# Finishing and storing each projection tile behind its own norms in a two-layer hybrid decoder step

## The reference, cut to what matters

```python
def project(xn, pos, p):
    z = xn @ p['w_in']                       # 1088 x 1024 by 1024 x 2448
    qa, ka, va, fa, glu_in, qc, kvc, gc, ud, vd = jnp.split(z, SPLIT_IDX, axis=-1)
    qa = rmsnorm(qa, p['fox_qn_g']);  ka = rmsnorm(ka, p['fox_kn_g'])
    logf = jax.nn.log_sigmoid(fa + p['fox_bf'])
    glu = ga * jax.nn.sigmoid(gb)
    qc = rope(rmsnorm(qc, p['nsa_qn_g']), pos)
    keys = rope(rmsnorm(kvc[:, :, 0::2], p['nsa_kn_g']), pos)
    gc = jax.nn.sigmoid(gc)
...
o_a = fox_prompt(qa, ka, va, logf)           # attention with a running sum of logf
o_b = conformer_conv(glu, ...)               # 31 taps along the rows, channel by channel
o_c = nsa_prompt(qc, gc, kvc, p)             # compressed, selected and window attention
o_d = gmlp_gate(ud, vd, p)                   # u * (lower triangle of ws @ layernorm(v) + bs)
y = merge_and_ffn(x, (o_a, o_b, o_c, o_d), p)
```

## Time and profile before

| | us |
|---|---|
| median of 3 runs | 4176.93 (4174.57 to 4179.18) |
| the profiled execution | 4181.78 |
| its span in the trace | 4179.9 |
| PE busy in the span | 3425.3 (82%) |
| DVE busy | 1442.6 (35%) |
| ACT busy | 977.6 (23%) |
| mean granted clock of PE | 0.911 |

### The profile page before, as it was taken

The page is one execution under the profiler, slowest core; times in us unless marked ns, Lnnn a source line. Parts: engine busy times, 40 slices in busy tenths (PEclk is TensorE's granted clock), DMA queues, the critical chain, the costliest instruction groups (busy, mean ns, idle before and its releaser), DMA issues.

```text
span 4179.9 us, 56173 instructions
## 1 busy us (share of the span) xinstructions
PE 3425.3 (82%) x22454; PEld 1933.6 (46%) x22454; DVE 1442.6 (35%) x2646; ACT 977.6 (23%) x1745; POOL 165.7 (4%) x136
## 2 busy tenths in 40 slices
PE   6987848888357999999988885688882779999998
PEld 3444436566223444444444443466661334444444
DVE  2555433333442321232127454333344333212311
ACT  2111114444222320121011111244442122102301
POOL 0111110000000000000001111000000000000000
PEclk8998869999778999999999897799996889999999
DMA  6322162332210121111072223433303111201211
GB/s 209 90 69 87 46 174 79 112 127 75 89 42 25 45 65 30 37 54 50 20 203 63 75 72 92 118 127 112 125 23 102 33 32 49 61 20 50 60 50 43
DMA packets 407740, 317.19 MB, mean 76 GB/s; under 512 B 158493, under 2 KB 389562, under 8 KB 400186
## 3 DMA queue, kind: packets, MB, share of 16 engines
q1 hardware_dynamic: 400490, 213.65, 18.5%
q0 software_dynamic: 7072, 101.19, 6.9%
HBM read 272.27 MB, written 51.84 MB: 78 GB/s over the span
## 4 chain that ended last, share of the span: by engine, by line
PE 65%; SPq 8%; DVE 8%; issue 7%; ACT 5%; DMA 5%; POOL 1%; POOLq 0%; DVEq 0%; ACTq 0%
PE PS L887 39%; PE PS L977 5%; PE PS L1240 4%; PE PS L1221 4%; PE PS L905 3%; PE PS L1122 2%; PE PS L879 2%; DMA out_fox_logf_p<-arena 2%; POOL arena L2360 1%; SPq L710 1%; PE PS L967 1%; PE PS L1163 1%; PE PS L1254 1%; ACT arena L1424 1%; SPq L705 1%
## 5 line engine op out<-in xcount | busy, mean ns | idle before, releaser
L887 PE MATMUL PS<-arena 128*128 128x512 bf16 (+1 forms) x10368 | 1634.7, 319 | 74.9 <-DVE arena L1698 40.0
L887 PEld LDWEIGHTS PS<-arena 128*128 128x128 bf16 x10368 | 789.5, 98 | 919.5 <-issue 93.3
L977 PE MATMUL PS<-arena 128*128 128x512 f32 (+3 forms) x1152 | 482.1, 574 | 0.9 <-ACT arena L1399 0.9
L1375 ACT ACTIVATE arena<-arena 128x1024 bf16<-128x1024 f32 (+1 forms) x112 | 145.5, 1301 | 1268.7 <-PE PS L887 1155.5
L2268 DVE TENSOR_TENSOR arena<-PS,arena 128x1088 f32 (+1 forms) x48 | 62.1, 1293 | 778.2 <-PE PS L887 778.2
L977 PEld LDWEIGHTS PS<-arena 128*128 128x128 f32 (+1 forms) x1152 | 208.8, 185 | 239.0 <-issue 204.5
L1969 DVE TENSOR_REDUCE arena<-PS 128x1 f32<-128x1024 f32 (+5 forms) x192 | 138.8, 724 | 379.4 <-PE PS L1224 379.3
L1221 PE MATMUL PS<-arena 128*128 128x512 f32 (+3 forms) x576 | 231.5, 509 | 5.7 <-ACT arena L1489 4.4
L2301 DVE SCALAR_TENSOR_TENSOR arena<-PS,arena 128x1088 f32<-128x1088 f32 x64 | 82.7, 1293 | 388.6 <-PE PS L887 388.6
L1240 PE MATMUL PS<-arena 128*128 128x64 f32 x1632 | 216.5, 279 | 0.0
L1240 PEld LDWEIGHTS PS<-arena 128*128 128x128 f32 x1632 | 204.1, 197 | 8.3 <-issue 5.0
(11 more groups left out here) (311 smaller groups left out, 2784.8 us busy)
## 6 DMA issues: line engine op xcount, KB each, us to landing
arena<-in_w_ff SPq DMA_DIRECT2D x64, 512.0 KB, 4.1
arena<-in_w_ff SPq DMA_DIRECT2D x32, 1024.0 KB, 5.6
arena<-in_cache_nsa_kv SPq DMA_DIRECT2D x256, 64.0 KB
x_s<-arena SPq DMA_DIRECT2D x2, 4352.0 KB, 18.1
arena<-x_s SPq DMA_DIRECT2D x2, 4352.0 KB, 13.3
arena<-in_w_in SPq DMA_DIRECT2D x4, 2048.0 KB, 11.6
arena<-in_w_out SPq DMA_DIRECT2D x16, 512.0 KB, 4.2
arena<-o_s SPq DMA_DIRECT2D x48, 128.0 KB, 2.4
```

Source lines behind the costliest of these rows:

```text
L887: last = mm(PS[:, 1536 * k + a:1536 * k + a + wd], ww[:, c, :], xx[:, c, a:a + wd], start=c == 0 and n == 0, stop=c == blocks - 1 and n == 2)
L977: last = mm(PS[0:r, c * 512:c * 512 + b - a], XNT[:, j, t * P:t * P + r], Wt[:, j, a:b], start=j == 0, stop=j == KD - 1)
L1375: run(WH[k][:, 0:blocks, :], WF[k][:, 0:blocks, :], ACT.Copy).then_inc(S["w_hi"], 1)
```

## The change

Six edits, as the diff shows them:

1. DVE's step for tile t becomes `norm_rows(t)`, `finish(t)`. PE's `small(t - 1)` moves from the end of its step t to the middle, between the product and the transposes of that step's two pieces, and ACT's `compressed_in(t - 1)` and some wait counts follow it.
2. SP stores tile t in step t. The store of `y_s` is put ahead of tile 7's stores.
3. ACT's waits for the stores and for `fin` move from the head of the tile to the instruction ahead of which they stand now.
4. Two of a tile's three taps go between the row sums and the wait for the fourth chunk in `norm_rows`, the third goes into `rstd`, where DVE waits for POOL.
5. The four loads of keys and values become one load of `KV4` with runs of 1 KB, and the gate load goes behind head 0's loads. Transposes, `KTS` and the value products read and write that layout.
6. `fox_in(0)` moves ahead of the barrier, behind waits for `y_out` and for the last piece product.

```diff
@@ layout
-        KK = lo.take(QT * 2 * HD, t=QT, g=2, d=HD)
-        VV = lo.take(QT * 2 * HD, t=QT, g=2, d=HD)
-        KTS = [x.rearrange("p t g d -> p (t g d)") for x in (KK[:, 0:QT // 2], KK[:, QT // 2:QT])]
+        KV4 = lo.take(QT * 4 * HD, t=QT, g=4, d=HD)
+        KTS = [KV4[:, 4 * n:4 * n + 4, 0:3:2, :] for n in range(2)]
@@ SP
                 def store_step(t, k, m):
-                    if not (isinstance(t, int) and t == 0):
-                        store_tile(t - 1, 1 - k)
+                    if t == QT - 1:
+                        sp.wait_ge(S["conv_done"], CW)
+                        sp.dma_start(y_s, Yc.rearrange("p c n -> p (c n)")).then_inc(S["y_out"], 16)
+                    store_tile(t, k)
 
                 each_tile(store_step)
-                sp.wait_ge(S["conv_done"], CW)
-                sp.dma_start(y_s, Yc.rearrange("p c n -> p (c n)")).then_inc(S["y_out"], 16)
-                store_tile(8, 0)
...
-                for dst, first in ((KK, 2), (VV, 3)):
-                    for g in range(2):
-                        sp.dma_start(dst[:, :, g, :], kvc_s[0:SEQ, first + 2 * g, :].rearrange("(t p) d -> p t d", p=P)).then_inc(S["kv4_in"], 16)
+                sp.dma_start(KV4.rearrange("p t g d -> p t (g d)"),
+                             kvc_s[0:SEQ, 2:6, :].rearrange("(t p) g d -> p t (g d)", p=P)).then_inc(S["kv4_in"], 16)
+                head_in(0)
                 sp.dma_start(GH, g_s[0:SEQ].rearrange("(t p) c -> p t c", p=P)).then_inc(S["gate_in"], 16)
-                head_in(0)
@@ PE
                     if t < QT:
-                        pe.wait_ge(S["raw_ev"], 2 * (2 * t + 4) if t < QT - 1 else 2 * PIECES + 1)
+                        pe.wait_ge(S["raw_ev"], 2 * (2 * t + 3) if t < QT - 1 else 2 * PIECES + 1)
...
-                    if p >= 4:
-                        pe.wait_ge(S["cp_ev"], p // 2 - 1)
+                    if p >= 3:
+                        pe.wait_ge(S["cp_ev"], (p - 1) // 2)
...
                         elif t < QT and c == 2:
                             piece_mm(2 * t)
+                            if t:
+                                small(t - 1, 1 - k)
                             piece_T(2 * t + 1)
+                        elif t == QT and c == 2:
+                            small(t - 1, 1 - k)
...
-                    if t:
-                        small(t - 1, 1 - k)
@@ ACT
-                    if t >= 2:
-                        act.wait_ge(S[f"st{k}"], 176 * m)
-                        act.wait_ge(S["fin"], t - 1)
...
                     out(0, SQ[0:r, 0:512], 0, 512, ACT.Square)
+                    if t >= 2:
+                        act.wait_ge(S[f"st{k}"], 176 * m)
                     out(1, VB[k][0:r, :], 0, 260)
...
                     out(2, SQ[0:r, 764:1152], 0, 388, ACT.Square)
+                    if t:
+                        compressed_in(t - 1)
                     if t < QT:
                         piece_out(2 * t + 1)
+                    if t >= 2:
+                        act.wait_ge(S["fin"], t - 1)
                     out(3, UV[k][0:r, :], 0, 512)
...
-                    if t:
-                        compressed_in(t - 1)
@@ DVE
-            def rstd(out, sums, count, which, n):
+            def rstd(out, sums, count, which, n, meanwhile=None):
                 V.tensor_scalar(out, sums, 1.0 / count, EPS, ALU.mult, ALU.add).then_inc(S[f"{which}_mean"], 1)
+                if meanwhile:
+                    meanwhile()
                 dve.wait_ge(S[f"{which}_rstd"], n)
...
                     V.reduce_sum(SS18[0:r, 0:18], SQ[0:r, :].rearrange("p (g d) -> p g d", d=HD), AX)
+                    taps = list(range(FIRST_TAPS + t * TAPS, min(CW, FIRST_TAPS + (t + 1) * TAPS)))
+                    for j in taps[:-1]:
+                        conv(j)
...
-                    rstd(SS18[0:r, :], SS18[0:r, :], HD, "row", t + 1)
+                    rstd(SS18[0:r, :], SS18[0:r, :], HD, "row", t + 1, lambda: [conv(j) for j in taps[-1:]])
...
                     norm_rows(t, k, m)
-                    if t:
-                        finish(t - 1, 1 - k)
-                    for j in range(FIRST_TAPS + t * TAPS, min(CW, FIRST_TAPS + (t + 1) * TAPS)):
-                        conv(j)
+                    finish(t, k)
@@ POOL
                 G.tensor_scalar(piece_rows, piece_rows, POOL * PIECES, None, ALU.add)
+                pool.wait_ge(S["y_out"], 16)
+                pool.wait_ge(S["kvc_mm"], PIECES + 1)
+                fox_in(0)
                 everyone()
...
-                fox_in(0)
                 pool.wait_ge(S["suf_out"], 16 * NB)
```

More of the change, by code:

```diff
@@ L1028, in extra @@
                     if what == "kv":
-                        transposes(key, KK[:, :, key[1] // 2, :], HD, key[1] % 2)
+                        transposes(key, KV4[:, :, key[1] // 2 * 2, :], HD, key[1] % 2)
                     elif what == "q":
@@ L1138, in request @@
                             for c in range(4):
-                                last = mm(out[32 * c:32 * (c + 1), 0:P], QNALL[:, b, :], KTS[s % 2][:, c * P:(c + 1) * P],
+                                last = mm(out[32 * c:32 * (c + 1), 0:P], QNALL[:, b, :], KTS[s % 2][:, c],
                                           start=True, stop=True)
@@ L1189, in merged @@
                     last.then_inc(S["pt_T"], 1)
-                pe.wait_ge(S["kv4_in"], 64)
+                pe.wait_ge(S["kv4_in"], 16)
                 for n in range(4):
@@ L1238, in values @@
                     for n, j in enumerate(js):
-                        v = {"fox": VF[h % 2][:, j, :], "sel": VV[:, j, 0, :], "win": VV[:, j, 1, :]}[kind]
+                        v = {"fox": VF[h % 2][:, j, :], "sel": KV4[:, j, 1, :], "win": KV4[:, j, 3, :]}[kind]
                         last = mm(PS[:, at:at + HD], PTR[u % 2][:, n * P:(n + 1) * P], v,
@@ L1496, in request_out @@
                         n = key[2]
+                        src = group_bank(key)
                         dst = KTF[n // 2 % 2][:, n % 2, :] if n < 8 else KTS[n % 2]
-                        run(dst, group_bank(key), ACT.Copy).then_inc(S["pt_evA"], 1)
+                        if n >= 8:
+                            src = src.rearrange("p (t g d) -> p t g d", t=4, g=2)
+                        run(dst, src, ACT.Copy).then_inc(S["pt_evA"], 1)
                     elif key[2] < 2:
@@ L1887, in _ @@
                 each_tile(z_step)
-                finish(8, 0)
                 dve.wait_ge(S["kvc_mm"], PIECES + 1)
@@ L2158, in _ @@
                 V.memset(MX, -3e38)
-                dve.wait_ge(S["gate_in"], 16)
                 for key in GROUPS[:10]:
@@ L2166, in _ @@
                     h, v = u // UH_, u % UH_
-                    if v == 0:
+                    if v == 4:
+                        dve.wait_ge(S["gate_in"], 16)
                         V.tensor_copy(GU[h % 2][:, :, 1:3], GH[:, :, 3 * h + 1:3 * h + 3]).then_inc(S["dve_done"], 1)
@@ L2386, in _, with fox_in @@
                 G.tensor_scalar(piece_rows, piece_rows, POOL * PIECES, None, ALU.add)
+                def fox_in(b):
+                    G.indirect_dma_start(KVP[b % 2].rearrange("p r n -> p (r n)"), None,
+                                         A["cache_fox_kv"].rearrange("l n (q r) c h d -> (l n q) (r c h d)", r=NPG),
+                                         bass.IndirectOffsetOnAxis(block_rows[:, b:b + 1], 0)).then_inc(fox_in_sem[b % 2], 16)
+                pool.wait_ge(S["y_out"], 16)
+                pool.wait_ge(S["kvc_mm"], PIECES + 1)
+                fox_in(0)
                 everyone()
@@ L2400, in _ @@
                 pool.wait_ge(S["page_next"], 1)
-                def fox_in(b):
-                    G.indirect_dma_start(KVP[b % 2].rearrange("p r n -> p (r n)"), None,
-                                         A["cache_fox_kv"].rearrange("l n (q r) c h d -> (l n q) (r c h d)", r=NPG),
-                                         bass.IndirectOffsetOnAxis(block_rows[:, b:b + 1], 0)).then_inc(fox_in_sem[b % 2], 16)
-                fox_in(0)
                 pool.wait_ge(S["suf_out"], 16 * NB)
```

## The result

The changed kernel takes 4023.89 us (median of 4 runs, 4022.78 to 4026.89), the kernel before 4178.06 in the same comparison (4174.57 to 4179.84): a ratio of 0.9633, with a 95% interval of 0.9616 to 0.9650, so 3.7% faster. The forecast was 4026.

| us, from the traces | layer 0 projection | layer 0 attention | layer 1 projection | layer 1 attention |
|---|---|---|---|---|
| before | 389.5 | 548.4 | 390.7 | 557.3 |
| after | 327.3 | 535.8 | 327.3 | 540.1 |
| shorter by | 62.2 | 12.6 | 63.4 | 17.2 |

The account below looks back on a forecast made before the run. Late stores were taken to bound the projection stage, PE waiting: about 44 us a tile for 33 of work. 2 x 62.2 + 26 = 150.4 off the profiled 4181.8 gives 4031.4, less 4.9 for the median: 4026 us; range 4006 to 4058.

Parts of the forecast that it names:

- period of a tile: Projection stage: piece products follow each other at 33.3 us, PE's own work without a wait, where a tile cost about 44.
- DVE's statistics of tile 8: End of the projection stage: they start at 443.6 us, 0.7 after PE's last chunk ends at 442.9.
- first store of tile 8: End of the projection stage: the stores start at 461.4 us, where they began at 523.65 before.
- from there to the first load: Tile 8's stores to the attention stage's first load: left at 13.7 us, `y_s` store gone, last part of `fox_in(0)` in.
- a layer's projection stage: Time up to the attention stage's first load: 62.2 us a layer less, bounds 57 and 65.
- SP's stretch to `head_in(1)`: Attention stage's start: SP's queue ends 12.8 us earlier in layer 0, 14.3 in layer 1, from fewer loads and no stall.
- attention stages together: Both layers' attention starts: 26 us less, between 4.2 with none of SP's stall gone and 27.1 with all.
- layout and gates: KV4, `KTS` and gate wait in the attention stage: taken as 0, layout bounded at -8 to +8 us.
- PE as the bound: Projection stage: the loop through DVE, ACT and PE takes 29.3 us, under PE's 33.3, with 4 to spare.
- Rival A: Attention stage's start gives back only SP's 2.1 us twice, the stall coming from small packets' count; 4048 us, chance 0.14.
- Rival B: DVE's tap and POOL's power run one after the other: 4030 us, chance 0.20; both also slowed: 4052, chance 0.05.
- Rivals C and D: Late cache pieces stop PE, slower than before, chance 0.02; the fill fails, a tile costs 36 to 40 us, chance 0.05.

Follow-up runs that it names:

- e5: Changed kernel with four 256 KB loads of keys and values into KV4 and the gate load ahead of head 0's again; 4026.96 us, ratio 0.9617.
- e9: Changed kernel with each tile's third tap replaced by two one-input row sums under POOL's power; 4023.52 us, ratio 0.9631.
- e10: Changed kernel with each tap's two short instructions ahead of its two long ones; 4033.63 us, ratio 0.9656.
- e1: Changed kernel with all three taps of a tile behind `finish(t)`, none in a gap; 4022.55 us, ratio 0.9624.
- e7_two_more: Changed kernel with two more DVE instructions (about 1.35 us each) behind the two taps of tiles 0 to 6; 4029.50 us, ratio 0.9650.
- e3: Changed kernel with PE's `small(t - 1)` and ACT's `compressed_in(t - 1)` back at the end of step t; 4143.69 us, ratio 0.9912.
- e4: Changed kernel with ACT's waits for stores and `fin` back at the head of the tile; 4026.87 us, ratio 0.9615.
- e6: Kernel before with only the taps' new places in the two gaps, `finish` and stores late; 4188.31 us, ratio 1.0025.
- e2: Changed kernel with the 4 MB load of request 0, `fox_in(0)`, back behind the barrier; 4062.06 us, ratio 0.9716.
- e11: Changed kernel with 20 small loads on ACT's queue and SP's order at the attention stage's start changed, 2 MB bias copy early; 4020.48 us, ratio 0.9625.
- e7_four_more: Changed kernel with four more DVE instructions (5.4 us in all) behind the two taps of tiles 0 to 6; 4078.56 us, ratio 0.9765.

## Why the prediction was right

The steps in its order, forecast and measured in the trace after:

| step | forecast | measured |
|---|---|---|
| first piece product of tile 1 | 201.9 | 201.43 |
| period of a tile | 33.3 | 33.29 |
| DVE's statistics of tile 8 | 443.6 | 443.29 |
| first store of tile 8 | 461.4 | 461.21 |
| from there to the first load | 13.7 | 12.73 |
| a layer's projection stage | 62.2 less | 62.2 and 63.4 less |
| SP's stretch to `head_in(1)` | 12.8 and 14.3 less | 11.1 and 16.4 less |
| attention stages together | 26 less | 29.8 less |
| layout and gates | 0 | 0 within the scatter (e5) |

The exact hit on layer 0's projection stage is luck in part. The positions count from the start of the span, and the stage began 1.2 us earlier than before; from its own start, tile 8's statistics came 0.9 us late, and the way from tile 8's stores to the first load was 1.0 shorter. One small slip lies in the sum: 443.4 less 1 is 442.4, and the prediction goes on with 442.9; the last chunk ended at 442.5.

*PE as the bound.* Right, and tested from both sides. Taking 1.0 us a tile out of the loop (the power in e9 and e10) gains nothing. Adding 2.1 (e1) costs nothing, and adding 2.7 (e7_two_more) only the 2 us of tile 1; adding 5.4 costs 2.3 of period. The room was therefore 3.1 us; the prediction had 4, and its power without a tap beside it was 1.0 short. DVE's 8 us of waiting a tile is not that room: between DVE's last release and PE's `small` lie ACT's evacuation and the piece product, which wait too.

*What the gain comes from.* The prediction laid it to the stores. e3 shows that their earlier issue has to come with the move of `small`: without it 57 of 62 us a layer are gone again, because PE asks for `small(t - 1)` only at the step's end and DVE, in order, holds the next tile's norms behind it. e4 and e1 show that edits 3 and 4 carry nothing in this version, and e6 that edit 4 by itself costs 4 us in the stages that it touches (10 in the median, 5 to 16 by the interval). The other half, `small` moved but the stores a step late, was not run, and edit 3 was tried only where PE is the bound.

*Start of the attention stage.* Right in cause (e2), and mis-sized: 26 forecast, 29.8 measured, with 12.6 and 17.2 in place of 12.8 and 14.3. SP's queue shows where the sizes were off. In layer 1 of the kernel before, the stall did not end with the four issues that the prediction counted:

```profile
2607.58 13.55 SPq L691 DMA_DIRECT2D arena<-qa_s  x4
...
2622.92 2.04 SPq L688 DMA_DIRECT2D arena<-g_s  x1
...
2625.00 4.03 SPq L691 DMA_DIRECT2D arena<-qa_s  x4
```

The last two take 0.31 and 1.35 in layer 0, so 4.4 us more were held there, in part behind the landing of the 4 MB load (2625.4); by what is not shown. Against that, edit 5 saved SP 1.6 us up to the small loads in layer 0, not 2.1. What is left, 29.8 for SP's 27.5, is not told from the scatter of the stage. Rival A (the count of packets) is refuted by e2. What e2 adds is that the edit is worth more than the stall it removes from the kernel before: 37 us, since without it the stall grows to 20.97.

*Rival B.* Half true. Tap and power do disturb each other, but for 1.0 us, not 2.9, and only the power is held. The Trainium skill, page "SBUF — State Buffer", section "Who interferes with whom", says that a VectorE instruction with two inputs from SBUF contends with a GpSimd instruction that reads SBUF, and that one with a single input, outside the modes that use both ports, does not. e9 (3.39 us beside one input) agrees. The section calls the contention an exclusive lock, and says of the modes that use both ports that whoever issues first has the pair for its whole instruction. Read so for the tap, as the prediction did, it agrees with POOL waiting out the running tap, 0.98 us; that the power then keeps DVE out for its 3.4 us does not come out: four instructions of DVE take 2.87 beside it and 2.89 without it.

*Rivals C and D.* PE waits for no piece in any tile, and no tile is over 33.3.

The forecast lies 2 us from the median, closer than its parts, and that is luck: two errors cancel. Against the profiled execution the sum of the savings was 6.7 us short (4031.4 for 4024.69): 1.2 in layer 1's projection stage, 3.8 in the attention stages, 1.6 elsewhere. The 4.9 us then taken off for the way from the profiled execution to the median were 0.8 in the changed kernel.

## What to carry to other kernels

Where engines hand work round in a ring and one of them runs its list in order, look at the place in its list where it takes what the others wait for: here undoing the move of a 1.5 us block on PE lost nearly all of the projection stage's gain, and new places for DVE's fill work and for ACT's waits carried none. Measure the room of the loop that is not the bound by adding known work to it; the idle time of one of its engines overstates it. Look in the issuing queue for loads that take many times their usual time to issue, and at which large load is in flight beside them. Put that one where the queue has nothing else to issue (e2: 37 us), and expect that another order may only move the stall (e11).

## What the runs showed of the hardware

- With a 4 MB indirect load under way, SP's issues of four loads of 256 B took 12.05, 13.55 and 20.97 and 18.69 us (e2), against 1.34 without it, and these issues ended 2.6 to 4.6 us ahead of the load's landing. With a copy of 2 MB and such a load both under way, one load of 264 KB took 15.35 and 15.22 us to issue (e11), while page loads of 64 KB in the same place took 1.6 each (changed kernel). The cost is in the issuing queue, and whatever stands behind it is late by as much.
- A gap of PE costs more than its length in some cases only: in e7_four_more tiles are 2.3 us longer in four cases of six and 4.7 in two. In one tile of each sort PE waits 2.3 us, with a granted clock of 1.00 in the first and 0.91 in the second. In e3 gaps of 6.8 us cost another 2.6 in slower matmuls, at a granted clock of 0.50 in the one that is shown.
- POOL's power of 19 columns: 3.4 us alone and beside one-input work, 4.37 when a 1.28 us instruction with two inputs had just begun, 3.40 when a 0.28 us one had.
